# Eight rounds of the last token tile's choice of keys, moved from the value projection into the first half of the attention

## The chip, the cores and the metric

One core of one Trainium2 chip runs the whole program. The metric is device time in microseconds (us). The core's engines run side by side and meet through semaphores: PE (TensorE matmuls), PEld (its weight loads), DVE (VectorE), ACT (ScalarE), POOL (GpSimd) and the DMA queues.

## The reference

Two transformer blocks for 512 tokens of width 1024, in float32: a gated linear attention with a mixture of experts, then an S5 mixer with a dense feed-forward part, then sparse attention with a second one. The change lies in the sparse attention. There, cut to what matters:

```python
score = jnp.einsum('bqhk,bqh->bqk', jax.nn.relu(s_idx), wb)   # 8 index heads
score = jnp.where(causal, score, -jnp.inf)
_, sel = lax.top_k(score, topk)                               # topk = 128
logits = jnp.einsum('bqhd,bqkhd->bhqk', qb, kg).astype(f32) * att_scale
logits = jnp.where(valid, logits, -jnp.inf)
p = jax.nn.softmax(logits, axis=-1).astype(vg.dtype)
return jnp.einsum('bhqk,bqkhd->bqhd', p, vg)                  # 16 heads of 64
```

Each query keeps 128 keys of those at or before it. The 512 queries form four tiles of 128 (t = 0 to 3); tile 0 keeps all its keys, so a choice is made for tiles 1, 2 and 3.

## The kernel before

**The choice.** DVE keeps a score per key in `bias[t]`, 256, 384 or 512 columns wide for t = 1, 2, 3. One round of the choice is MAX8 (L2550: the eight largest of each row) and MATCH_REPLACE (L2551: those eight are marked as taken). Sixteen rounds choose 128 keys; after the sixteenth, L2553 turns marks into a bias of 0 or -1e30. Three tiles make 48 rounds, in the order of tiles. `choose(n)` issues the next n of them at the place where it stands in DVE's program. Nothing but that placement sets their order; DVE works its program off in order, and so do ACT and PE.

**The projections.** A loop over s = 0 to 22. For s up to 20 PE projects one block of index queries, keys or queries, and turns it by the rotary tables (job `rot`, finished by DVE at L2577 and L2580). Steps 21 and 22 are the value projection: each is 96 matmuls of 512 columns, in four halves of 24 (L348, job `dv`). A weight half must be split in two parts before PE uses it: ACT makes the high part (L708), DVE the low part (L716, 128x1024), PE waits for the low part. There are two buffers, used by turns, so ACT may write half g only when PE has begun half g-1, and DVE follows ACT. In steps 21 and 22 DVE goes four times through `weights_low_part` and then `choose`. The two halves that PE starts with in step 21 have been split before; so the first of the four calls splits nothing, and the second splits the third half of the projection.

**The attention.** Each of 64 steps takes one pair (tile, head). Steps 0 to 31 alternate two heads of tile 1 and two of tile 2; the later ones take tiles 0 and 3, the first of tile 3 at step 34. For step s

- PE issues, in this order: the transpose `pt` of pair s-3 (L1370), the product with the values `av` of pair s-4 (L1383), the logits `lg` of pair s (L1392). After the logits of steps 0 to 3 it also issues one filling matmul (L1398) and waits for its end.
- DVE adds the bias to the logits and takes the maximum (L2630, then L2633), in odd steps scales the outputs of pair s-4 (L2600, L2602), and in some steps makes a round of the choice.
- ACT takes the exponential of pair s-1 (L1824), then copies the transpose of pair s-3 out of PSUM (L1834), which `av` of the next step needs.

So the logits of pair s, once DVE has taken their maximum, hold up ACT's exponential, behind that ACT's copy of pair s-2's transpose, and behind that PE's `av` in step s+2. After the attention come the output projection and the second feed-forward part.

Of the kernel before, what the change touches and what calls it, by code (L numbers as in the profile page):

```python
# [140 lines left out]
NR = len(ROPED)  # L141
# [27 lines left out]
NPAIR = len(PAIRS)  # L169
# [223 lines left out]
def block_kernel(nc, io, out, scratch):  # L393

    with ExitStack() as ctx:
# [173 lines left out]
        def free(name):  # L569
            return bank_free[JOBS[name] % 8]  # L570
# [1276 lines left out]
        def _(dve):  # L1847
# [693 lines left out]
            def choose(n):  # L2541

                for _ in range(n):
                    t, at = 1 + chosen[0] // (TOPK // 8), chosen[0] % (TOPK // 8)
                    if t == NTX:
                        return
                    chosen[0] += 1
                    if at == 0:
                        dve.wait_ge(S["b_masked"], t + 1)
                    link(nc.vector.max(m8[:], bias[t]))  # L2550
                    link(nc.vector.match_replace(bias[t], m8[:], bias[t], TAKEN))  # L2551
                    if at == TOPK // 8 - 1:
                        link(nc.vector.tensor_scalar(bias[t], bias[t], TAKEN / 2, MASKED, ALU.is_gt, ALU.mult))  # L2553

            for s in range(NR + 2):
                if s >= NR:
                    for q in range(4):
                        weights_low_part(dve, half_of("dv", s - NR, KT, True) - 2 + q, split_to)
                        choose(4 if s == NR else 3)
                if 1 <= s <= NR and ROPED[s - 1][2] == "tile":  # L2560
                    m = tiles_normed.index(s - 1)
                    dve.wait_ge(S["b_rroot"], norm_index[s - 1] + 1)
                    link(nc.vector.reciprocal(rst[:, m % 2, :], rst[:, m % 2, :]))
                    gain = ROPED[s - 1][3]
                    dve.wait_ge(S["b_raw_ready"], s)
                    nc.vector.scalar_tensor_tensor(out=roped_tile(s - 1), in0=roped_tile(s - 1),
                                                   scalar=1.0 if gain is None else col("qk_gain", gain),
                                                   in1=rst[:, m % 2, :], op0=ALU.mult, op1=ALU.mult) \
                        .then_inc(S["b_normed_q"], 1)
                    dve.wait_ge(S["b_normed_q"], m + 1)  # L2570
                if s < NR:
                    weights_low_part(dve, ahead("dv", ROPED[s][0], ROPED[s][1]), split_to)
                if s >= 2:
                    name = f"rot{s - 2}"
                    ps = result(dve, name)
                    v = roped_tile(s - 2)
                    link(nc.vector.tensor_tensor(rt[:, 0, :], ps[:], cossin[:, 1, :], ALU.mult))  # L2577
                    dve.sem_inc(free(name), 1)
                    dve.wait_ge(S["b_turned_cos"], s - 1)
                    nc.vector.tensor_tensor(v, v, rt[:, 0, :], ALU.add).then_inc(S["b_rotated"], 1)  # L2580
                    dve.wait_ge(S["b_rotated"], s - 1)
                if s == 6:
                    ps = result(dve, "wi")
                    link(nc.vector.tensor_scalar(wi, ps[:, 0:NTX * IH].rearrange("p (t h) -> p t h", h=IH),
                                                 float(IH) ** -0.5, float(HD) ** -0.5, ALU.mult, ALU.mult))
                    dve.sem_inc(free("wi"), 1)
                if s < NR:
                    for t, i in indexed_at(s):
                        index_score(t, i)
                    if s >= INDEX_FIRST + 5:  # L2590
                        choose(4)
# [29 lines left out]
            for s in range(NSTEP):  # L2621
                if s < NPAIR:
                    t, h = PAIRS[s]
                    w = (t + 1) * P
                    b = s % 4
                    name = f"lg{s}"
                    ps = result(dve, name)
                    if s >= 4:
                        dve.wait_ge(bank_done, JB[f"pt{s - 4}"] + 1)
                    link(nc.vector.tensor_tensor_reduce(pp[:, b, 0:w], ps[:, 0:w], bias[t], 1.0, -3.0e38,  # L2630
                                                        ALU.add, ALU.max, mx[:, b:b + 1]))
                    dve.sem_inc(free(name), 1)
                    nc.vector.tensor_scalar(nmx[:, b:b + 1], mx[:, b:b + 1], rsq[:, t, h:h + 1], -1.0, ALU.mult,  # L2633
                                            ALU.mult).then_inc(S["b_logits"], 1)
                if VALUE_LAG <= s < NPAIR + VALUE_LAG and (s - VALUE_LAG) % 2 == 1:
                    outputs_scaled(s - VALUE_LAG)
                if s in TILE_DONE:
                    mixed_low(TILE_DONE[s])
                if s < NPAIR // 2 and s % 4 == 1:
                    choose(1)  # L2640
            assert chosen[0] == (NTX - 1) * (TOPK // 8)
            for j in range(KT):
# [90 lines left out]
```

## Time and profile before

| | |
|---|---|
| runs | 3161.42, 3164.7 and 3247.57 us, median 3164.7 |
| the profiled execution's own time | 3160.65 us |
| its span (first to last instruction) | 3158.8 us, 1.85 us less than its time |
| PE busy | 2900.4 us, 92% of the span |
| DVE busy | 1864.0 us, 59% |
| ACT busy | 1393.9 us, 44% |
| value projection | from 2525.8 to 2579.5 us |
| attention | from 2580.4 to about 2720 us |
| rounds of the choice | from 2513.9 to 2646.3 us |

A timeline row gives start and duration in us, engine, line, operation, output and inputs, the number of instructions, and in brackets how long the engine had sat idle and what ended that. All instants are us from the start of the span.

### The profile page before, as it was taken

To read this page: it belongs to the slowest core of one execution; us is meant where nothing else is said; L and a number is where in the kernel's file an instruction comes from. 1 tells how busy PE (TensorE), PEld (TensorE's weight loads), DVE (VectorE), ACT (ScalarE), POOL (GpSimd) and SP (SyncE) were. 2 spreads that over 40 slices of the span, in tenths; PEclk is the share of its full clock that TensorE was granted. 3 is DMA by queue.
4 is the path that set the end of the run, shared out by engine and by line. 5 is a ranking of instruction groups with operands and counts; after the bars stand their busy time and mean duration, and the time that the engine had idled before them with its cause. 6 is when DMAs were issued, how large, how long until landed. Compare 5 with 4: busy or idle time off the path is not lost.

```text
span 3158.8 us, 35772 instructions
## 1 busy us (share of the span) xinstructions
PE 2900.4 (92%) x12800; PEld 2235.7 (71%) x12800; DVE 1864.0 (59%) x2206; ACT 1393.9 (44%) x1794; POOL 219.7 (7%) x167
## 2 busy tenths in 40 slices
PE   7999999985899999999993678999989999989998
PEld 2548878765677777777772566788867767768887
DVE  3435653564988888888887753333236685343322
ACT  2323233223667777777775323323223435333221
POOL 1100100003930000000001000000001100000000
PEclk9999999996999999999997879999999999999999
DMA  6921722314899989999993802222221110122221
GB/s 236 330 76 60 282 85 94 121 62 161 319 331 352 387 351 387 361 377 369 369 372 108 107 32 75 94 95 106 93 75 67 67 54 1 41 72 101 94 94 67
DMA packets 90801, 546.92 MB, mean 173 GB/s; under 512 B 9232, under 2 KB 18848, under 8 KB 32384
## 3 DMA queue, kind: packets, MB, share of 16 engines
q1 hardware_dynamic: 79584, 485.65, 41.6%
q0 software_dynamic: 10816, 59.58, 5.5%
q8 instruction: 74, 1.21, 0.2%
q14 instruction: 39, 0.32, 0.0%
q10 hardware_dynamic: 288, 0.15, 0.0%
HBM read 516.51 MB, written 41.42 MB: 177 GB/s over the span
## 4 chain that ended last, share of the span: by engine, by line
PE 69%; DVE 17%; issue 6%; DMA 4%; ACT 3%; SPq 1%; POOL 1%; DVEq 0%; ACTq 0%; PEldq 0%; POOLq 0%
PE bank L348 38%; PE bank L286 6%; PE bank L1138 5%; PE bank L1142 4%; PE bank L1141 4%; DVE expert_low L2218 4%; DMA arena<-in_we_stream 2%; ACT expert_high L1587 1%; PE bank L1370 1%; PE bank L1392 1%; PE bank L1383 1%; DMA arena<-in_mod 1%; PE bank L1122 1%; DVE expert_x_low L2303 1%; DVE arena L2320 1%
## 5 line engine op out<-in xcount | busy, mean ns | idle before, releaser
L2218 DVE TENSOR_TENSOR expert_low<-arena,expert_high 128x2048 fp32r<-128x2048 f32 x291 | 684.2, 2382 | 102.7 <-ACT expert_high L1587 85.4
L1587 ACT ACTIVATE expert_high<-arena 128x1024 fp32r<-128x1024 f32 x582 | 597.2, 1057 | 213.4 <-PE bank L1138 117.5
L348 PE MATMUL bank<-high_b,weight_parts 128*128 128x512 f32 x1872 | 592.9, 398 | 29.6 <-DVE low_b L2456 15.9
L716 DVE TENSOR_TENSOR weight_parts<-ring_pages,weight_parts 128x1024 fp32r<-128x1024 f32 x185 | 226.7, 1226 | 557.9 <-ACT weight_parts L708 557.4
L708 ACT ACTIVATE weight_parts<-ring_pages 128x1024 fp32r<-128x1024 f32 x185 | 196.1, 1060 | 591.6 <-PE bank L348 552.4
L348 PEld LDWEIGHTS bank<-high_b,weight_parts 128*128 128x128 f32 x1872 | 352.8, 190 | 121.1 <-issue 36.3
L348 PE MATMUL bank<-low_b,weight_parts 128*128 128x512 f32 x832 | 325.7, 391 | 0.0
L1138 PE MATMUL bank<-expert_high,expert_x_low 128*128 128x512 f32 x768 | 309.5, 403 | 14.1 <-DVE expert_low L2218 10.4
L1141 PE MATMUL bank<-expert_high,expert_x_high 128*128 128x512 f32 x768 | 301.1, 392 | 0.0
L1142 PE MATMUL bank<-expert_low,expert_x_high 128*128 128x512 f32 x768 | 300.6, 391 | 0.0
L348 PE MATMUL bank<-hidden_parts,weight_parts 128*128 128x512 f32 x1056 | 240.0, 389 | 4.3 <-DVE hidden_parts L2502 4.3
L348 PEld LDWEIGHTS bank<-hidden_parts,weight_parts 128*128 128x128 f32 x1056 | 198.0, 188 | 46.3 <-DVE hidden_parts L2502 5.2
L348 PE MATMUL bank<-high_x,parts_a 128*128 128x512 f32 x640 | 202.9, 399 | 9.0 <-DVE parts_a L716 8.6
L1138 PEld LDWEIGHTS bank<-expert_high,expert_x_low 128*128 128x128 f32 x768 | 144.7, 188 | 68.7 <-DVE expert_low L2218 38.2
L348 PEld LDWEIGHTS bank<-low_b,weight_parts 128*128 128x128 f32 x832 | 157.4, 189 | 32.8
L1138 PE MATMUL bank<-expert_high,expert_h_low 128*128 128x512 f32 x384 | 156.2, 407 | 17.5 <-DVE expert_low L2218 15.1
L1142 PEld LDWEIGHTS bank<-expert_low,expert_x_high 128*128 128x128 f32 x768 | 144.9, 189 | 31.8
L1141 PEld LDWEIGHTS bank<-expert_high,expert_x_high 128*128 128x128 f32 x768 | 145.2, 189 | 28.1
L1142 PE MATMUL bank<-expert_low,expert_h_high 128*128 128x512 f32 x384 | 150.3, 391 | 0.0
L1141 PE MATMUL bank<-expert_high,expert_h_high 128*128 128x512 f32 x384 | 149.8, 390 | 0.0
L348 PEld LDWEIGHTS bank<-high_x,parts_a 128*128 128x128 f32 x640 | 122.1, 192 | 35.9 <-issue 9.7
L348 PE MATMUL bank<-high_b,parts_a 128*128 128x512 f32 x320 | 126.7, 396 | 0.0
(464 smaller groups left out, 4033.2 us busy)
## 6 DMA issues: line engine op xcount, KB each, us to landing
arena<-in_we_stream SPq DMA_DIRECT2D x294, 1024.0 KB, 6.5
ring_pages<-in_wb_stream SPq DMA_DIRECT2D x93, 1024.0 KB, 4.8
ring_pages<-in_wa_stream SPq DMA_DIRECT2D x49, 1024.0 KB, 4.9
arena<-in_mod POOLq DMA_DIRECT2D x16, 1024.0 KB
xbuf<-arena POOLq DMA_DIRECT2D x25, 512.0 KB, 15.9
arena<-xbuf SPq DMA_DIRECT2D x17, 512.0 KB, 7.3
ybuf<-arena SPq DMA_DIRECT2D x16, 512.0 KB, 2.6
arena<-kd SPq DMA_DIRECT2D x8, 512.0 KB, 24.1
```

The lines of the kernel that those rows point to most:

```text
L286: ins = pe.matmul(o, lhsT, rhs, start=start, stop=stop)
L348: ins = pe.matmul(o, lhsT, rhs, start=start, stop=stop)
L708: nc.scalar.activation(high, src, ACT.Copy).then_inc(weights_high, 1)
L716: nc.vector.tensor_tensor(low, src, high.bitcast(F32), ALU.subtract).then_inc(weights_split, 1)
L1122: ins = pe.transpose(ps[:, q * P:(q + 1) * P], parts[:, q * P:(q + 1) * P], ident[:])
L1138: ins = pe.matmul(o, low, w_high, start=start, stop=False)
L1141: pe.matmul(o, high, w_high, start=False, stop=False)
L1142: return pe.matmul(o, high, w_low, start=False, stop=stop)
L1370: ins = pe.matmul(ps[:, b * P:(b + 1) * P], pp[:, k % 4, b * P:(b + 1) * P], ident[:], start=True, stop=True)
L1383: ins = pe.matmul(av[:, c:c + HD], pT[:, k % 2, b * P:(b + 1) * P], vt[:, b, h * HD:(h + 1) * HD], start=(b == 0), stop=(b == t))
L1587: nc.scalar.activation(ehigh[c % HIGH_E][:, at], ring_e[c % RING_E][:, at], ACT.Copy) \
L2218: nc.vector.tensor_tensor(elow[c % RING_E][:], ring_e[c % RING_E], ehigh[c % HIGH_E][:].bitcast(F32), ALU.subtract).then_inc(weights_split ...
```

## The change

Two numbers in DVE's program. Before, steps 18, 19 and 20 made 4 rounds each, step 21 four times 4, step 22 four times 3, and the attention one round in steps 1, 5, ..., 29. Now step 21 makes four times 2, and the attention makes a round in every odd step up to 31. In all there are 48 as before.

```diff
@@ -2556,7 +2556,7 @@
                 if s >= NR:
                     for q in range(4):
                         weights_low_part(dve, half_of("dv", s - NR, KT, True) - 2 + q, split_to)
-                        choose(4 if s == NR else 3)
+                        choose(2 if s == NR else 3)
@@ -2636,7 +2636,7 @@
                     outputs_scaled(s - VALUE_LAG)
                 if s in TILE_DONE:
                     mixed_low(TILE_DONE[s])
-                if s < NPAIR // 2 and s % 4 == 1:
+                if s < NPAIR // 2 and s % 2:
                     choose(1)
```

DVE at the start of the value projection, as the first difference between the two programs; L716 here is the low part of the third half (128x256 are rounds of tile 1).

```order
 L2550 MAX m<-arena 128x8
 L2551 MATCH_REPLACE arena<-m,arena 128x256
+L716 TENSOR_TENSOR weight_parts<-ring_pages,weight_parts 128x1024
 L2550 MAX m<-arena 128x8
 L2551 MATCH_REPLACE arena<-m,arena 128x256
```

The third half's low part now stands two rounds of tile 1, and the L2553 that ends them, earlier.

DVE at the end of the value projection, a piece of the difference (128x512 are rounds of tile 3).

```order
-L716 TENSOR_TENSOR weight_parts<-ring_pages,weight_parts 128x1024
-L2550 MAX m<-arena 128x8
-L2551 MATCH_REPLACE arena<-m,arena 128x512
-L2550 MAX m<-arena 128x8
-L2551 MATCH_REPLACE arena<-m,arena 128x512
-L2550 MAX m<-arena 128x8
-L2551 MATCH_REPLACE arena<-m,arena 128x512
 L2577 TENSOR_TENSOR arena<-bank,arena 128x512
 L2580 TENSOR_TENSOR arena<-arena 128x512
```

All eight rounds of tile 3 are gone from here; tile 2's last round now stands ahead of L2577.

DVE in an odd step of the attention that had no round before; the same piece comes again every four steps.

```order
 L2600 RECIPROCAL rsm<-sm 128x2
 L2602 TENSOR_TENSOR arena<-bank,rsm 128x128
+L2550 MAX m<-arena 128x8
+L2551 MATCH_REPLACE arena<-m,arena 128x512
 L2630 ISA arena,mx<-bank,arena 128x256
```

The round stands between the scaling of outputs and the next step's logits.

## Rows read from the trace of the kernel before

**Rows 1.** The page: busy time of PE and the others, share, instructions.
```profile
PE 2900.4 (92%) x12800; PEld 2235.7 (71%) x12800; DVE 1864.0 (59%) x2206; ACT 1393.9 (44%) x1794; POOL 219.7 (7%) x167
```

**Rows 2.** Timeline of PE around the value projection (columns as told above).
```profile
2542.48 0.80 PE L348 MATMUL bank<-weight_parts,low_p 128*128 128x512 f32 x1 [5.24 <-DVE weight_parts L716]
...
2547.62 0.40 PE L348 MATMUL bank<-weight_parts,low_p 128*128 128x512 f32 x1
...
2585.30 1.12 PE L1398 MATMUL bank<-arena,ident 128*128 128x512 f32 x2
2587.94 0.71 PE L1370 MATMUL bank<-ident,arena 128*128 128x128 f32 x4 [1.52 <-ACT arena L1824]
```

**Rows 3.** Timeline of DVE around the value projection.
```profile
2532.99 0.43 DVE L2550 MAX8 m<-arena 128x8 f32<-128x256 f32 x1
...
2541.20 1.23 DVE L716 TENSOR_TENSOR weight_parts<-ring_pages,weight_parts 128x1024 fp32r<-128x1024 f32 x1
...
2579.66 0.70 DVE L2550 MAX8 m<-arena 128x8 f32<-128x512 f32 x1
...
2581.18 0.69 DVE L2550 MAX8 m<-arena 128x8 f32<-128x512 f32 x1
...
2584.21 0.69 DVE L2577 TENSOR_TENSOR arena<-bank,arena 128x512 f32<-128x512 f32 x1
...
2586.36 0.42 DVE L2630 CUSTOM_DVE_ANT_0 arena<-bank,arena 128x256 f32<-128x256 f32 x1
```

**Rows 4.** Timeline of ACT around the value projection.
```profile
2532.06 1.06 ACT L708 ACTIVATE weight_parts<-ring_pages 128x1024 fp32r<-128x1024 f32 x1 [4.34 <-PE bank L348]
2543.38 1.06 ACT L708 ACTIVATE weight_parts<-ring_pages 128x1024 fp32r<-128x1024 f32 x1 [10.25 <-PE bank L348]
```

**Rows 5.** Windows of PE: stretch, length, busy, granted clock, DMA share, GB/s.
```profile
431.50:434.50 3.00, 3.00 (x8) 0.50 0.82 330
```
**Rows 6.** The same view, of the value projection.
```profile
2542.50:2547.00 4.50, 4.50 (x11) 0.50 0.61 233
```

**Rows 7.** Timeline of PE, two other gaps.
```profile
430.43 0.70 PE L348 MATMUL bank<-high_x,parts_a 128*128 128x512 f32 x2 [2.75 <-DVE parts_a L716]
...
434.85 0.63 PE L348 MATMUL bank<-high_x,parts_a 128*128 128x512 f32 x2
```
**Rows 8.** Timeline of PE, a shorter gap.
```profile
2217.24 3.02 PE L348 MATMUL bank<-hidden_parts,weight_parts 128*128 128x512 f32 x12 [2.17 <-DVE hidden_parts L2502]
```

**Rows 9.** Windows of all engines, four steps of the attention: PE, PEld, DVE, ACT, POOL, clock.
```profile
2617.10:2625.25 8.15, 8.15 (x50) 6.02 (x49) 5.03 (x19) 4.27 (x13) 0.00 (x0) 1.00 0.01 2
```

**Rows 10.** Timeline of DVE, steps 15 to 18 of the attention.
```profile
2616.34 0.29 DVE L2602 TENSOR_TENSOR arena<-bank,rsm 128x128 f32<-128x128 f32 x1
2617.15 0.42 DVE L2630 CUSTOM_DVE_ANT_0 arena<-bank,arena 128x256 f32<-128x256 f32 x1 [0.52 <-PE bank L1392]
...
2619.94 0.29 DVE L2602 TENSOR_TENSOR arena<-bank,rsm 128x128 f32<-128x128 f32 x1
2620.38 0.69 DVE L2550 MAX8 m<-arena 128x8 f32<-128x512 f32 x1
...
2621.89 0.56 DVE L2630 CUSTOM_DVE_ANT_0 arena<-bank,arena 128x384 f32<-128x384 f32 x1
```

**Rows 11.** Timeline of ACT, the same steps.
```profile
2618.58 0.47 ACT L1834 ACTIVATE arena<-bank 128x384 f32<-128x384 f32 x1
...
2623.57 0.36 ACT L1834 ACTIVATE arena<-bank 128x256 f32<-128x256 f32 x1
```

**Rows 12.** Timeline of PE, `av` of steps 18, 20 and 32.
```profile
2619.70 0.78 PE L1383 MATMUL bank<-arena 128*128 128x64 f32 x6
...
2623.98 0.66 PE L1383 MATMUL bank<-arena 128*128 128x64 f32 x4
...
2648.89 0.66 PE L1383 MATMUL bank<-arena 128*128 128x64 f32 x4 [0.38 <-ACT arena L1834]
```

**Rows 13.** Timeline of DVE, the end of tile 3's choice.
```profile
2646.34 0.43 DVE L2553 TENSOR_SCALAR arena<-arena 128x512 f32<-128x512 f32 x1
```

## The prediction

> **What bounds the kernel now.** I read the page first: PE is busy for 92% of the span [rows 1], so a change on DVE is worth what it takes from, or adds to, PE's few idle stretches. Then I read the timelines of PE, DVE and ACT from 2500 to 2660 us, where all rounds of the choice lie, and looked for each place where PE's idle time ends with something that DVE did.
>
> There are two near the value projection. PE has worked off two weight halves at 2537.24 (2542.48 less the 5.24 us of idle time in brackets), and waits those 5.24 us for the low part of the third, which DVE starts at 2541.20 and ends at 2542.43 [rows 2, 3]. ACT had made the high part from 2532.06 to 2533.12 [rows 4]: neither the transfer nor ACT is what is late, it is DVE, which from 2532.99 on made eight rounds first. Then PE, at the start of the attention, comes to its first transpose when its last filling matmul ends at 2586.42 and waits 1.52 us for the first exponential, which waits for DVE's first logits at 2586.36 [rows 2, 3]. DVE has no idle time there, it comes straight from tile 3's rounds.
>
> In the attention PE has no idle time: four steps take 8.15 us, PE is busy in all of them and DVE in 5.03 [rows 9]. By its busy share DVE has room for one more round in four steps. What a share does not show is when the round falls. That I read from the starts below.
>
> **Term 1, the stall for the third half.** The low part now stands behind six rounds instead of eight. Six of eight rounds of tile 1 take (2541.20 - 0.33 - 2532.99) x 6/8 = 5.91 us, so it starts at 2538.90, where 0.33 is the last of the eight followed by L2553 (about 0.3 us for 256 columns by the 0.43 of 512 [rows 13]). That is 2.30 us earlier, and PE starts the half at 2540.18. **-2.3 us.** The later halves wait for ACT, which waits for PE: the fourth half's high part began 0.90 us after PE began the third [rows 2, 4], took 1.06, and DVE's low part takes 1.23: some 3.3 us with the hand-overs, where a half of 24 matmuls takes PE 24 x 0.227 = 5.4. With two or three rounds (2.5 to 3.8 us) between the low parts, DVE is in time for every one of them, so the gain is kept to the end of the projection. DVE will have idle time in the first half of it, which costs nothing.
>
> **Term 2, the clock behind that stall.** In the gap the granted clock falls to 0.50, its lower level of 1.2 GHz [rows 6], and PE needs 5.14 us for the 12 matmuls from 2542.48 to 2547.62 [rows 2]; at the upper level they take 12 x 0.227 = 2.72 (0.227 from three in 0.68 us). So 2.4 us are lost. The new gap is 2540.18 - 2537.24 = 2.94 us. The nearest rows are a gap of 2.75 us, after which the clock was at 0.50 too, and twelve matmuls took 4.42 us, from 430.43 to 434.85, 1.7 more than at the upper level [rows 5, 7]; and a gap of 2.17 us, after which 12 matmuls took 3.02 including the last one's tail, at the upper level throughout [rows 8]. 2.94 is nearer to 2.75 and beyond it, so I take 1.7 lost instead of 2.4: **-0.7 us.** The ends are 0 lost (-2.4) and 3.4 lost, twice as long at the low level (+1.0).
>
> The Trainium skill ("TensorE: Matmul & The Clock Gate", section "Why this matters for your kernels") advises short idle gaps between bursts of matmuls, so that the clock is not taken back, and by its advice the shortened gap would just pass. By that rule the clock term would be the end of -2.4, not -0.7. The row of the 2.75 us gap speaks against it, that of 2.17 us for it.
>
> **Term 3, the first exponential.** Without tile 3's eight rounds (1.52 us each, from 2579.66 to 2581.18 [rows 3]) DVE would be at its first logits 12.2 us sooner; but L2577 ahead of them waits for PE's last rotation, which comes 3.0 us sooner by terms 1 and 2. From there DVE has L2577, L2580, a reciprocal, 2586.36 - 2584.21 = 2.15 us in all, and starts the logits at about 2580.5, 5.9 us before its former time. Exponential and hand-overs take 2587.94 - 2586.36 = 1.58 us, so PE could have it at 2582.1, and comes to it at 2586.42 - 3.0 = 2583.4. The wait goes: **-1.5 us.** Here PE would be 4.5 us ahead of before.
>
> **Term 4, the eight rounds in the attention.** Steps 1, 5, ... have had theirs; new are steps 3, 7, ..., 31. Look at step 15. DVE scales outputs at 2616.34 and is free for a round 0.44 us later (2619.94 to 2620.38 in the step that has one); the round holds it for 1.51 (2620.38 to 2621.89) [rows 10]. The next logits, ready at 2617.15, then start at 2616.34 + 0.44 + 1.51 = 2618.29: 1.14 us late. ACT's exponential waits for them, and behind it in ACT's order its copy, which before ended at 2618.58 + 0.47 = 2619.05, ends at 2620.19 [rows 11]. PE's `av` of step 18 began at 2619.70 [rows 12] and needs that copy; with a hand-over of 0.06 it begins at 2620.25. PE is late by **0.55 us**. That this coupling is real can be seen twice before the change: the round of step 17 makes the copy end at 2623.93 and `av` begin at 2623.98; and where L2553 follows the last round (0.46 us more), PE stands idle 0.38 us at 2648.89 [rows 11 to 13].
>
> The lag does not pile up on DVE (it stays ahead of PE over four steps), but each such round sets PE back anew. Steps 7, 11, 15, 19, 23 and 27: 6 x 0.55 = 3.3 us. Step 3 has a filling matmul behind it and no outputs to scale, which covers its round: 0. Step 31 has the last round and L2553: its next logits are late by 1.14 + 0.46 and, since tile 0's logits are ready some 0.2 to 0.3 us sooner, 1.9 in all; less the slack of 0.59 (2619.70 - 2619.05 - 0.06) that is 1.3, while the stall at 2648.89, with L2553 gone from step 29, goes (0.38 and a little over 0.1 of late start): +0.8. Together **+4.1 us**. The ends: 0, if ACT's copy had more room than the rows show; and 8 x 1.51 = 12.1, if nothing at all were covered. I take 4.1, since it comes from the starts themselves.
>
> **The sum.** -2.3 - 0.7 - 1.5 + 4.1 = -0.4 us, on the profiled execution's own 3160.65: 3160.2. Its time lies 0.8 us under the lowest and 4.05 us under the median of the runs shown. From the lowest run, 3161.4, it is 3161.0. I take 3161.0 as the time to be measured. A measurement of this kernel can tell 2%, 63 us, from no change; no case below comes near it.
>
> **The rivals.**
>
> *The clock stays up* (as with the 2.17 us gap [rows 8]). -2.3 - 2.4 - 1.5 + 4.1 = -2.1: 3159.3. For it, that the gap shrinks by almost half; against it, the 2.75 us gap.
>
> *The rounds hide in the attention.* DVE is idle for 3.1 of 8.15 us [rows 9], and 1.51 fits in. If ACT's copy did not wait behind the exponential, the sum would be -4.5: 3156.9. Against it, the two places of rows 12 where PE already follows a late copy.
>
> *Slower: DVE's round sits whole in PE's path.* In the steps with a new round, DVE is 1.14 us late for the logits; if PE's transposes or the release of PSUM banks also waited for it, each of eight rounds would cost up to its whole 1.51 us: +12.1 - 4.5 = +7.6, 3169. It decides from the point where DVE's late logits are still late four steps on, that is if the four steps of DVE, 5.03 + 1.51 = 6.5 us of work and its hand-overs, took over 8.7. In between, at a cost of 1.14 for each of seven, +3.5: 3165.
>
> *The change does not do what it says:* the third half waits for something else, say the ring page or PE's own buffer. Then terms 1 and 2 are nothing, term 3 stays, and the sum is +2.6: 3164. Against it, ACT's high part done at 2533.12, nine microseconds early [rows 4].
>
> **How the numbers follow.** Forecast 0.55, clock up 0.15, rounds hidden 0.1, rounds wholly in the path 0.12 (most of it the milder price), no gain at the half 0.03; 0.05 for what I have not seen. The range reaches from the hidden rounds' 3156.9, a little lower for the spread between runs, to the milder slower case with 2 us of that spread: 3156.5 to 3167. It leaves out the 3169 case and most of what is unseen. Faster or slower by over 2% would need 63 us, for which no case has a mechanism: 0.01 and 0.02, the rest within.
>
> **What the profile of the changed kernel would show.** PE's gap in front of the third half about 2.9 us, still ended by L716 (term 1); granted clock 0.50 after it for a stretch shorter than before, or not at all (term 2). No idle time ahead of the first L1370 (term 3), and the last filling matmul some 3 us earlier. In the attention, idle time of PE of 0.5 to 0.65 us ahead of L1383, ended by ACT L1834, six times, 8.7 us (8.15 + 0.55) apart, and one of about 1.3 near step 34 (term 4); PE's lead over before shrinks from 4.5 us at step 9 to almost nothing at step 34, and stays so to the end. I am wrong if the lead at step 34 is over 2 us, or if PE's lag in four steps is over 1 us.

## The result, and the profile after

No difference of 2% from the kernel before can be told, and the time is not the one that was forecast. The ratio to the kernel before is 1.0076, with a 95% interval of 1.0051 to 1.0100. The median of 20 executions is 3197.3 us, outside the forecast range of 3156.5 to 3167.

This ratio can't be understood alone: the comparison leaves out executions more than 1.5% above the fastest of their kernel, and so leaves out those of before near 3247 us (12 of 20) but keeps those of the changed kernel near 3200 us (13 of 20). All executions taken together show this:

| | to 3180 us | 3180 to 3230 | over 3230 | mean of all |
|---|---|---|---|---|
| before, 20 beside the changed kernel | 8, median 3165.3 | 0 | 12, 3238 to 3257 | 3214.3 |
| changed, 20 | 7, median 3167.3 | 13, 3192 to 3207 | 0 | 3188.2 |
| before, all 167 of this study | 103, median 3164.3 | 2 | 62 | 3195.5 |

Each kernel, then, has two kinds of execution. The profile tells what the second kind is in the changed kernel. The page of the changed kernel, busy times and the granted clock in 40 slices, is of an execution of 3193.91 us:

```profile
span 3192.1 us, 35771 instructions
PE 2939.2 (92%) x12800; PEld 2262.0 (71%) x12800; DVE 1864.8 (58%) x2206; ACT 1395.3 (44%) x1794; POOL 219.5 (7%) x167
PEclk9999999996999999999998699999999996899999
```

PE is busy 39 us longer than in [rows 1], with as many instructions, and DVE for 0.8. PE's timeline shows the three places that the prediction spoke of: the third half, the first transpose, and `av` of steps 10, 14 and 34 (bracket: idle time and what ended it).

```profile
2539.27 0.50 PE L348 MATMUL bank<-weight_parts,low_p 128*128 128x512 f32 x1 [2.95 <-DVE weight_parts L716]
...
2543.70 0.39 PE L348 MATMUL bank<-weight_parts,low_p 128*128 128x512 f32 x1
...
2582.69 0.68 PE L1370 MATMUL bank<-ident,arena 128*128 128x128 f32 x4 [0.30 <-ACT arena L1824]
...
2586.57 0.70 PE L1392 MATMUL bank<-arena 64*128 64x256 f32 x2
...
2598.54 0.88 PE L1383 MATMUL bank<-arena 128*128 128x64 f32 x6 [0.38 <-ACT arena L1834]
...
2607.34 0.88 PE L1383 MATMUL bank<-arena 128*128 128x64 f32 x6 [0.57 <-ACT arena L1834]
...
2647.50 0.48 PE L1392 MATMUL bank<-arena 64*128 64x128 f32 x2
...
2651.74 1.05 PE L1383 MATMUL bank<-arena 128*128 128x64 f32 x6 [1.14 <-ACT arena L1834]
...
2676.02 1.95 PE L1370 MATMUL bank<-ident,arena 128*128 128x128 f32 x8
```

Against the kernel before this trace starts the stall 0.91 us sooner (2542.48 - 5.24 against 2539.27 - 2.95, the last digit rounded), for reasons that lie ahead of the change. With that taken off, PE is 2.3 us ahead at the third half, and 5.40 - 0.91 = 4.5 us ahead at the logits of step 4 (2591.97 before, 2586.57 now), as forecast. At `av` of step 34 (2652.34 before, 2651.74 now) the lead has been used up and 0.3 us more. From there to the end of the program the changed kernel loses 33.9 us, and all of it before the output projection, whose first matmuls start 33.3 us later (first line before, second now) behind the same wait of 1.89 us:

```profile
2726.11 0.74 PE L348 MATMUL bank<-high_b,weight_parts 128*128 128x512 f32 x2 [1.89 <-DVE low_p L2616]
```
```profile
2759.40 0.74 PE L348 MATMUL bank<-high_b,weight_parts 128*128 128x512 f32 x2 [1.89 <-DVE low_p L2616]
```

No new wait does it. Windows of the changed kernel, the first three of PE alone (length, busy, granted clock, DMA share, GB/s): behind the stall for the third half, in the first half of the attention, and behind `av` of step 34. The last two, of all engines in the second half of the attention, give PE, PEld, DVE, ACT, POOL and then the clock:

```profile
2540.20:2543.00 2.80, 2.80 (x8) 0.50 0.97 328
...
2600.00:2640.00 40.00, 37.54 (x221) 1.00 0.01 1
2654.00:2664.00 10.00, 9.34 (x31) 0.50 0.01 2
```
```profile
2680.00:2700.00 20.00, 20.00 (x70) 15.39 (x70) 5.08 (x25) 6.92 (x21) 0.00 (x0) 0.50 0.01 1
2700.00:2720.00 20.00, 20.00 (x66) 14.87 (x66) 5.07 (x24) 5.99 (x18) 0.00 (x0) 0.50 0.00 1
```

and of the kernel before (all engines):

```profile
2680.00:2700.00 20.00, 19.67 (x114) 14.29 (x112) 9.05 (x42) 11.08 (x33) 0.00 (x0) 1.00 0.01 1
```

The clock was granted at 0.50, the level of 1.2 GHz, right behind the gap of 1.14 us, came back for some steps, and fell again, to the end of the attention, at the transposes of 2676.02 us: eight matmuls that start there take 1.95 us, those at 2666.74 took 1.16. At 0.50 PE works off 70 matmuls in 20 us instead of 114. In the trace of the kernel before the clock stays at 1.00 through the attention.

### The profile page after: what moved, and what is told of

It reads as the page before. It is cut to its first block, busy times and chain, and to the rows that moved or that the text cites. A ratio compares the mean times of both kernels' runs of the same rounds, so it can differ in the third digit from the quotient of the medians.

```text
span 3192.1 us, 35771 instructions
## 1 busy us (share of the span) xinstructions
PE 2939.2 (92%) x12800; PEld 2262.0 (71%) x12800; DVE 1864.8 (58%) x2206; ACT 1395.3 (44%) x1794; POOL 219.5 (7%) x167
## 4 chain that ended last, share of the span: by engine, by line
PE 70%; DVE 16%; issue 6%; ACT 3%; DMA 3%; SPq 1%; POOL 0%; DVEq 0%; ACTq 0%; PEldq 0%; POOLq 0%
PE bank L348 40%; PE bank L286 6%; PE bank L1138 4%; DVE expert_low L2218 4%; PE bank L1142 4%; PE bank L1141 4%; DMA arena<-in_we_stream 2%; PE bank L1392 2%; ACT expert_high L1587 1%; PE bank L1370 1%; PE bank L1383 1%; PE bank L1122 1%; DVE expert_x_low L2303 1%; DVE arena L2320 1%; PE bank L1194 1%
## 5 line engine op out<-in xcount | busy, mean ns | idle before, releaser
L716 DVE TENSOR_TENSOR weight_parts<-ring_pages,weight_parts 128x1024 fp32r<-128x1024 f32 x185 | 226.7, 1226 | 561.3 <-ACT weight_parts L708 560.9
```

The source lines that it names most:

```text
L716: nc.vector.tensor_tensor(low, src, high.bitcast(F32), ALU.subtract).then_inc(weights_split, 1)
```

## The experiments

Seventeen kernels ran, most of them 12 times, one (evenf2, again as evenf2b) twice 12 times. What is counted is the number of executions over 3180 us and over 3230 us; one over 3180 us is said to have fallen. In the traces kept, those from 3180 to 3230 us had a low clock in the second half of the attention, and the one over 3230 us, of proj, in the whole of it. No trace of the kernel before near 3247 us was kept; its executions there, beside the experiments, have a mean clock over the span of 0.924 to 0.932, like proj's 0.929; those to 3180 us have 0.954 to 0.962. "Even rounds" is the version with `s % 2 == 0` for `s % 2` in the attention.

The expectations name their theories by letters. G: idle gaps of PE bring the clock down. A: the sparse steps, with tile 0's small matmuls, do it by themselves. P: it hangs on where in time these steps lie. M: it falls without regard to gaps. R: a round costs the same wherever it stands.

| kernel | runs | to 3180 (median) | 3180 to 3230 | over 3230 |
|---|---|---|---|---|
| before | 167 | 103 (3164.3) | 2 | 62 |
| changed | 20 | 7 (3167.3) | 13 | 0 |
| proj: term 1 alone | 12 | 9 (3165.9) | 0 | 3 |
| att: terms 3 and 4 | 12 | 7 (3166.4) | 5 | 0 |
| bfill: before + 1 filling matmul | 12 | 12 (3165.4) | 0 | 0 |
| bfill64: the same, other data | 12 | 11 (3163.6) | 1 | 0 |
| no31: last round in the projection | 12 | 8 (3163.6) | 4 | 0 |
| afterf2: changed + 2 filling | 12 | 7 (3170.2) | 5 | 0 |
| afteralt: changed, other order | 11 | 11 (3171.4) | 0 | 0 |
| less, lessf1: eight rounds left out | 6 and 6 | 0 | 12 | 0 |
| even rounds | 12 | 4 (3158.1) | 8 | 0 |
| evenf1, +1 filling | 12 | 8 (3159.5) | 4 | 0 |
| evenf2 and evenf2b, +2 filling | 24 | 22 (3163.7) | 2 | 0 |
| evenf3, +3 filling | 12 | 7 (3164.5) | 5 | 0 |
| even35, filling at step 35 | 12 | 7 (3161.9) | 5 | 0 |
| evenfill4, at 35, 41, 47, 53 | 12 | 5 (3161.8) | 7 | 0 |
| evenswap | 7 | 2 (3173.3) | 5 | 0 |
| evenalt: other order | 12 | 10 (3164.0) | 2 | 0 |

(One more execution of proj took 5877 us; it is unlike all others and not counted. The bound of 3180 us is a reading aid, and shorter falls lie under it: evenswap's execution of 3178.7 us had a low clock for 51 us, evenf2b's of 3174.7 us for about 30.)

The rows come from several chips, and on these the kernel before, run beside each row, was not alike: 15 of 30 over 3230 us beside proj, even, no31 and less; 10 of 30 beside bfill, evenswap, even35 and evenfill4; 9 of 30 beside evenf1, evenf2, lessf1 and att; 10 of 29 beside bfill64, afterf2 and evenf3; 6 of 28 beside evenalt, afteralt and evenf2b. A difference between rows of different groups may in part be one of chips.

**The first transpose and the executions near 3247 us.**

proj, term 1 without the rest:

```diff
-                        choose(4 if s == NR else 3)
+                        choose((2, 6, 4, 4)[q] if s == NR else 3)
```

> Term 1 alone, with all rounds in the projection that were there before: step 21 makes 2, 6, 4, 4 rounds instead of 4, 4, 4, 4, the attention is as before. The third half comes 2.3 us sooner, the fourth at its former time, so PE reaches the attention about 1.5 us sooner, but DVE its first logits at the former time, 2586.4. Expected: the gap of 1.5 us ahead of the first L1370 grows to about 3 us and the time stays at 3160.6, 0 us from before, where the clock stays up. Theory G: with a gap of 3 us at the beginning of the attention the clock falls there in at least as many executions as before, and such an execution loses most of the attention's 130 us at half clock: some 80 us, 3240. Rival M: no more and no fewer such executions than before.

Ratio 1.0003 (0.9992 to 1.0014). The third half came in time (gap 2.94 us), but two later gaps of 1.32 and 1.10 us took its place, both ended by L716, so PE came to the first transpose no sooner, with a gap of 1.51 us and not the 3 of the forecast. Term 1 alone is worth nothing. 3 of 12 were over 3230 us, where theory G had at least the share of the kernel before (15 of 30). Its profile, of an execution of 3250.9 us span, is the one in which the clock fell at the beginning. PE's timeline there, and the windows (all engines) of the stretch behind it:

```profile
2594.98 1.11 PE L1370 MATMUL bank<-ident,arena 128*128 128x128 f32 x4 [1.51 <-ACT arena L1824]
```
```profile
2596.00:2650.00 54.00, 53.70 (x170) 38.39 (x170) 17.57 (x67) 16.95 (x45) 0.00 (x0) 0.50 0.00 1
2650.00:2720.00 70.00, 70.00 (x230) 51.26 (x229) 22.87 (x87) 21.22 (x56) 0.00 (x0) 0.50 0.00 1
```

Four transposes that took 0.71 us in [rows 2] take 1.11: the clock is down right behind the gap, and stays at 0.50 for the whole attention, although PE is busy nearly all of the time.

bfill puts work into that gap:

```diff
     if _s < FILLED:
         JOBS_B += [f"fill{_s}"]
+    if _s == 2:
+        JOBS_B += ["fill2b"]
...
+                if s == 2:
+                    ps = opened("fill2b")
+                    pe.matmul(ps[:], ident[:], vt[:, 0, 0:512], start=True, stop=True).then_inc(bank_done, 1)
+                    pe.wait_ge(bank_done, JB["fill2b"] + 1)
+                    pe.sem_inc(free("fill2b"), 1)
```

> The kernel before with one filling matmul more, after the one of step 2, where PE waited 1.52 us for the first exponential: PE has 1.4 us of work in place of the wait, so the path does not change. Theory G (a gap of 1.5 us at the beginning of the attention brings the clock down for the whole of it): no execution near 3247 us is left of those that before had in half its cases (27 of 50); the best ones stay at 3160 to 3166 us. Where the clock then falls in the second half instead, an execution takes about 3195 us, as the changed kernel's do. Rival M (no tie to the gap): executions near 3247 us as often as with the kernel before.

Ratio 1.0013 (1.0004 to 1.0023); but 0 of 12 over 3180 us, with 12 of 30 of the kernel before on the same chip. PE's timeline (two filling matmuls in a row, then the transpose) and its windows:

```profile
2594.50 1.13 PE L1400 MATMUL bank<-arena,ident 128*128 128x512 f32 x2
2595.77 1.10 PE L1405 MATMUL bank<-arena,ident 128*128 128x512 f32 x2
2597.17 0.68 PE L1372 MATMUL bank<-ident,arena 128*128 128x128 f32 x4 [0.30 <-ACT arena L1831]
```
```profile
2596.00:2650.00 54.00, 53.40 (x307) 1.00 0.01 1
...
2669.20:2672.40 3.20, 3.17 (x15) 0.51 0.00 0
2673.00:2730.00 57.00, 56.23 (x339) 1.00 0.00 1
```

307 matmuls in 54 us where proj had 170. Behind the gap of step 36 the clock fell here too, but came back after some 3 us. In all, no kernel whose gap ahead of the first transpose was 0.9 us or less had an execution over 3230 us (0 of 206); those with 1.5 us had 65 of 179. It does not take a filling matmul: att and the changed kernel close the gap without one more (0 of 32). That much is shown: the gap of term 3 is what costs 80 us, in about a third of the executions, and closing it is worth far more than its 1.5.

**Where the rounds stand.**

att, the changed attention with the old third half:

```diff
-                        choose(2 if s == NR else 3)
+                        choose(4 if s == NR else 1)
```

> The attention of the changed kernel alone: sixteen rounds in its odd steps, but the eight are taken out of step 22 (four times 1 instead of 3), and step 21 keeps four times 4. The third half is as late as before (gap of 5.24 us), the first exponential is in time. By the terms: -1.5 (term 3) + 4.1 (term 4) = +2.6 us, 3163.3 us at a clock of 1.00, six gaps of 0.57 us and one of 1.14. No execution near 3247 us, since the gap of 1.52 us ahead of the first transpose is gone. How many fall in the second half tells whether it hangs on the inside of the attention (then as with the changed kernel, 13 of 20, theory G) or on its place (theory P: another share, as the attention begins 2.9 us later than in the changed kernel).

No execution over 3230 us, the best at 3162.0 and the median of seven at 3166.4, 0.7 above the 3165.7 of the kernel before on that chip, where 2.6 were forecast; in the second half the clock fell in 5 of 12. PE's waits from 2575 to 2660 us (total, times, longest):

```profile
PE bank L1383 <- ACT arena L1834: 4.6, 7, 1.1
```

The same line, with the same numbers, stands in the changed kernel's waits: term 4's seven gaps, without term 1. In this trace, of 3168.9 us, the clock stayed at 1.00 behind the gap of 1.14 us, behind which it fell in the changed kernel's.

even, the sixteen rounds moved by one step:

```diff
-                if s < NPAIR // 2 and s % 2:
+                if s < NPAIR // 2 and s % 2 == 0:
```

> The sixteen rounds of the attention in its even steps (0, 2, ..., 30) instead of the odd ones; the projection as in the changed kernel. Theory G (the gaps): PE's 0.57 us gaps come from rounds that stand in front of the logits of steps 8, 12, ...; in an even step there is no scaling of outputs ahead of the round, so the logits of the next step are late by 0.3 us at most and ACT's copy is in time. Expected: gaps ahead of L1383 gone but for one of about 0.6 us at step 33, PE 4.7 us ahead of before at step 34, and, since no gap of 1.1 us is left in the attention, a granted clock of 1.00 through it: 3156 us. Rival R (term 4 is too small because rounds cost DVE time wherever they stand): same gaps, 3161 us. Rival M (the clock falls in the attention without regard to gaps): gaps gone, but many executions near 3190 us or more as before.

The gaps went, as expected. PE's waits there:

```profile
PE bank L1392 <- DVEq L759: 1.1, 1, 1.1
PE bank L1383 <- ACT arena L1834: 0.8, 2, 0.5
```

The four executions to 3180 us have a median of 3158.1 against 3164.1 of before's: 6.0 us less, where 4.7 were worked out. In the trace PE needs 63.97 us from the first transpose to `av` of step 34 (2582.94 to 2646.91), before 64.40 (2587.94 to 2652.34). So the rounds cost PE nothing in an even step: rival R is out. But the clock fell all the same, in 8 of 12, as M had it and against G (one gap of 1.11 us was left, at step 36, which the kernel before has too). In its profile PE stands idle nowhere for over 0.35 us between 2653.36 and the fall:

```profile
2665.69 0.48 PE L1392 MATMUL bank<-arena 64*128 64x128 f32 x2
2666.10 1.96 PE L1370 MATMUL bank<-ident,arena 128*128 128x128 f32 x8
```

These are the same transposes, of step 43, as at 2676.02 us in the changed kernel: tile 3's, behind four pairs of tile 0.

no31 takes away the gap in step 34:

```diff
-                        choose(2 if s == NR else 3)
+                        choose(2 if s == NR else 4 if q == 3 else 3)
...
-                if s < NPAIR // 2 and s % 2:
+                if s < NPAIR // 2 - 1 and s % 2:
```

> The changed kernel with the round of step 31, the last of all, made at the end of step 22 instead. Theory G: the 1.14 us gap ahead of L1383 in step 34 goes, replaced by nothing; the six gaps of 0.57 us stay. PE 1.4 to 1.5 us further ahead at step 34: 3159 us at a clock of 1.00. If the 1.14 us gap is what brings the clock down at 2652 us, no execution falls there any more and none lies near 3200 us. Rival M: executions near 3200 us stay as frequent as with the changed kernel (13 of 20), falling elsewhere.

The gap went, and one of 0.90 us ahead of the first transpose, not forecast, came, as DVE reached the attention 1.5 us later. 4 of 12 fell, against 13 of 20: fewer, yet the gap in step 34 is not the only cause (with so few executions the two shares are not far enough apart to be sure of more).

less leaves out the eight added rounds (tile 3 keeps 64 keys, L2553 follows its eighth round):

```diff
-                if s < NPAIR // 2 and s % 2:
+                if s < NPAIR // 2 and s % 4 == 1:
```

> The changed kernel without its eight additional rounds in the attention (rounds in steps 1, 5, ..., 29 only). It leaves out the last eight rounds of tile 3's choice, so that tile keeps only 64 keys; L2553 is still done. This is terms 1 to 3 alone. Theory G: 3160.65 - 4.5 = 3156 us, PE 4.4 us ahead of before at step 34, only gaps of 0.1 and one of 0.4 us in the attention, and a clock of 1.00 throughout. If it falls in the attention nonetheless, gaps are not what brings it down (rival M), and times near 3190 to 3240 appear.

6 of 6 fell, 3189 to 3202 us, though no gap of the added rounds was left. The forecast failed, and with it theory G as an account of the added gaps: whether these have a part in the 13 of 20 is not shown. Its windows of PE:

```profile
2590.00:2650.00 60.00, 59.14 (x350) 1.00 0.00 1
2661.00:2700.00 39.00, 39.00 (x132) 0.50 0.00 1
```

**Gap, sparse steps, place or data.**

evenswap, outputs scaled ahead of the logits:

```diff
             for s in range(NSTEP):
+                if VALUE_LAG <= s < NPAIR + VALUE_LAG and (s - VALUE_LAG) % 2 == 1:
+                    outputs_scaled(s - VALUE_LAG)
                 if s < NPAIR:
...
-                if VALUE_LAG <= s < NPAIR + VALUE_LAG and (s - VALUE_LAG) % 2 == 1:
-                    outputs_scaled(s - VALUE_LAG)
```

> Rounds in the even steps, and DVE scales the outputs of pair s-4 ahead of the logits of step s instead of behind them. In step 35 this frees the PSUM bank that the logits of step 36 wait for, so the gap of 1.11 us there (ended by DVE's release of a bank) should go or fall under 0.4 us, and the gap of 0.53 us in step 33 with it. At a clock of 1.00: 1 to 1.5 us less than the even rounds alone (best 3157.4), 3156. If the 1.11 us gap is what brings the clock down in the second half (theory G), the executions between 3184 and 3206 us (8 of 12 with the even rounds) become few; if low activity of the steps of tile 0 does it by itself (rival A), they stay about 2 in 3.

A miss. DVE now waited in odd steps for `av` of the same step before it could take the logits; with that, gaps of 0.60 and 0.95 us ahead of `av` came back, and behind the one of 0.95 the clock fell already in the first half:

```profile
2619.89 0.66 PE L1383 MATMUL bank<-arena 128*128 128x64 f32 x4 [0.95 <-ACT arena L1834]
...
2621.11 1.56 PE L1370 MATMUL bank<-ident,arena 128*128 128x128 f32 x6
```

even35 and evenfill4 put filling matmuls into the second half:

```diff
-    if _s < FILLED:
+    if _s < FILLED or _s == 35:
...
-                if s < FILLED:
+                if s < FILLED or s == 35:
```

(evenfill4: `in (35, 41, 47, 53)`.)

> Rounds in the even steps and one filling matmul after the logits of step 35, which takes PE 1.4 us where it waited 1.11 us: +0.3 us at a clock of 1.00, so the best executions at 3158. Theory G for the second half: executions over 3184 us become few, as PE is busy in the gap. Rival A: the clock still falls at the transposes of step 43, as it did in the profile of the even rounds (at 2666.1 us, no gap over 0.25 us in the 10 us ahead of it), and 2 of 3 executions stay between 3184 and 3206 us.

> Rounds in the even steps and a filling matmul after the logits of steps 35, 41, 47 and 53, so that each stretch of tile 0's small matmuls has 1.1 us of dense work: 4 x 1.4 us less the waits that they replace (1.1 and some 0.2 each), about +4 us at a clock of 1.00: 3161. Rival A (low activity of these steps brings the clock down): here the executions over 3184 us go or become few, and the median over all executions is near 3162. If they stay, neither the gap nor the sparse steps explain the fall.

5 and 7 of 12 fell, where the even rounds had 8. Filling the 1.11 us gap does not keep the clock, nor does dense work of 1.1 us between the sparse stretches. A window of even35 has PE recorded as busy without a break, at the low clock:

```profile
2666.00:2735.00 69.00, 69.00 (x216) 0.50 0.00 1
```

evenf1, evenf2, evenf3 and evenf2b move the attention later by one, two or three filling matmuls of 1.42 us after step 2 (names `fill2b`, `fill2c`, `fill2d` in the form of bfill's edit, on the even rounds):

> Rounds in the even steps and one filling matmul more after step 2, where PE waits for nothing any more: the whole attention from step 3 on comes 1.42 us later than with the even rounds, its inside is the same. Theory P (position): whether the clock falls in the second half depends on where in time its sparse steps lie, which is nearly the same in every execution; the change moved them 4.2 us forward, onto a bad place, and 1.4 us back brings them to where the kernel before with one more filling matmul had them (0 of 12 executions over 3173 us). Expected: 3157.5 + 1.4 = 3159 us for the best and nearly all executions under 3172 us, against 4 of 12 without the filling matmul. Theory G or A (gaps or sparse steps by themselves): 8 of 12 between 3184 and 3206 us as before, since no gap in the attention has changed.

> The same with two more filling matmuls: attention 2.84 us later than with the even rounds. At a clock of 1.00 3160.3 us. Theory P gives another share of executions over 3184 us than either 0 or 1 more (which, it does not say, as no kernel so far had this place); theories G and A give the same share as for the even rounds, 2 in 3.

> The even rounds with three more filling matmuls: 4.26 us later, so that the attention begins where it began in the kernel before, which fell in its second half in 2 of 43 of the executions that had not fallen at the first transpose. At a clock of 1.00: 3157.5 + 4.3 = 3162 us. Theory P: few or none over 3184 us. If the number of filling matmuls mattered through their work and not through the shift, also none; if neither, 2 in 3.

> The even rounds with two more filling matmuls once more. If the 0 of 12 over 3184 us is the kernel's own: again 0 or 1 of 12, median 3162 us. If it was chance out of a share like the 5 or 8 of 12 of its neighbours with three or none: 3 or more of 12.

With 0, 1, 2, 2 again and 3 of them 8, 4, 0, 2 and 5 of 12 fell. The inside of the attention, from the first transpose to `av` of step 34, is the same to 0.03 us. None against two (8 of 12 against 2 of 24) is far from chance, if the difference of the chips is left aside. So what lies ahead of the attention seems to matter; but that it is the place in time is not shown. Theory P forecast nearly none with one and with three, and 4 and 5 fell; evenf2b's 2 lie between its two forecasts; and its own trace has the clock low from 2690 to 2720 us. The instants speak against P too: the two traces of the same kernel, evenf2 and evenf2b, begin the third half at 2534.00 and 2538.17 us, and bfill and bfill64, alike up to there, at 2551.66 and 2543.45. The executions lie further apart than the shifts of 1.42 us, so a place counted from the start of the program cannot decide it. The filling matmuls are also more dense work, a rival that no run separates.

afterf2, the changed kernel with two:

> The changed kernel, rounds in its odd steps, with two more filling matmuls after step 2: the attention with all its gaps (six of 0.57 us, one of 1.14) comes 2.84 us later. At a clock of 1.00: 3160.2 + 2.8 = 3163 us. Theory P (place): far fewer than 13 of 20 over 3184 us, near the 0 of 12 of the even rounds with two. Theory G (gaps inside): as many as with the changed kernel, about 8 of 12.

5 of 12, against 2 of 24 with the gaps gone and 13 of 20 without the filling matmuls. The numbers are too small to say which of the two counts, or both.

lessf1 and bfill64. lessf1 is less with bfill's edit. bfill64 is bfill with

```diff
-                    link(nc.vector.match_replace(bias[t], m8[:], bias[t], TAKEN))
+                    link(nc.vector.match_replace(bias[t], m8[:], bias[t], TAKEN if t < 3 or at < 8 else -1.0e38))
```

> The changed kernel without its eight additional rounds in the attention (tile 3 keeps only 64 keys), and one filling matmul more after step 2. Without the filling matmul 6 of 6 executions lay between 3189 and 3202 us. Its attention is step for step that of the kernel before with one more filling matmul, only 2.8 us sooner in the program. Theory P: with the 1.42 us shift most executions come to 3158 to 3165 us. Theory G or A: 6 of 6 over 3184 us again.

> The kernel before with one more filling matmul, every instruction the same and at the same place, but the last eight rounds of tile 3 mark their keys with a value that does not count as taken: tile 3 keeps 64 keys instead of 128, so that more of its softmax weights are zero. Nothing but data differs. If data plays no part in the clock, executions lie at 3160 to 3173 us (0 of 12 over 3173 without this edit). If the sparser data makes the clock fall or stay down in tile 3's steps, most lie between 3187 and 3203 us, and the two kernels with rounds left out (6 of 6 there) are explained by their data and say nothing on gaps or place.

lessf1 fell 6 of 6, against theory P; bfill64 1 of 12. So the data, half of tile 3's keys, is not what made less and lessf1 fall. Up to `av` of step 34 the attentions of lessf1 and bfill64 differ by one wait of PE of 0.19 us, at 2633.64 us; what else differs lies ahead of the attention. In both the clock dips at step 36's gap for some 3 us and comes back; in lessf1 it falls again 10 us after that dip began (granted 1.00 from 2665 to 2671 us, 0.50 behind it). Why the one does and the other doesn't stays open.

evenalt and afteralt spread the small steps out:

```diff
-for _order in ((1, 2) * (AH // 2), (0, 3, 0) * (AH // 4) + (3,) * (AH // 4)):
+for _order in ((1, 2) * (AH // 2), (0, 3) * (AH // 2)):
```

> Rounds in the even steps, and the second half of the attention takes two heads of tile 0 and two of tile 3 by turns all the way, instead of four of tile 0 after two of tile 3 and eight pairs of heads of tile 3 at the end. Same work. Theory A (a stretch of four small pairs in a row brings the clock down): no execution over 3184 us, best ones 3156 to 3162 us. If the stretch is not what does it: about 8 of 12 over 3184 us as with the even rounds.

> The changed kernel with the same order of the second half. At a clock of 1.00 the gap of 1.14 us in step 34 stays, so 3160 to 3168 us. Theory A: few over 3184 us instead of 13 of 20. If the gaps that the rounds make (0.57 us six times, 1.14 us in step 34) are enough by themselves: about 8 of 12 over 3184 us.

2 of 23 over 3180 us, where the same kernels in the old order had 21 of 32. Neither forecast was met to the letter: evenalt has the 2 (3189.2 and 3195.7 us) where none was expected, and 7 of afteralt's 11 lie above its 3160 to 3168 us, up to 3178.7. In afteralt's profile the clock still fell behind the 1.14 us gap, and came back, but for one more dip of about 3 us at step 36. Its windows:

```profile
2659.00:2665.00 6.00, 6.00 (x21) 0.50 0.02 4
2673.00:2730.00 57.00, 55.50 (x326) 1.00 0.00 1
```

That fits a reading in which the gaps bring the clock down and the stretches of tile 0's small matmuls keep it down or let it fall again. For the falls of the second half it is the only forecast whose share held for both kernels. It is not shown beyond that: on the same chip evenf2b, in the old order, fell in 2 of 12 as well, the kernel before was over 3230 us least often there, and neither kernel ran in the old order without filling matmuls on that chip.

**A version better than both.** By the mean over all executions: bfill 3165.7 us (before in the same comparison 3192.5), evenf2 and evenf2b 3167.5 together (3189.4 and 3182.8), evenalt 3168.3 (3182.8), changed 3188.2 (3214.3). Among executions to 3180 us the even rounds are the fastest, with a median of 3158.1. None differs from before by 2%. The gain of all of them is that the executions near 3247 us don't occur; evenf2 and the spread order had, besides, few near 3195.

## Why the prediction was wrong

**Term 1, the stall: right.** Forecast -2.3; the gap is 2.95 us instead of 5.24.

**Term 2, the clock behind it: right in this trace, in part by luck.** The low level was there from 2540.2 to 2543.0 us; the first 12 matmuls of the third half take 4.43 us, from 2539.27 to 2543.70, against 2.72 at the upper level: 1.7 us lost, as I took. The rule of the Trainium skill ("TensorE: Matmul & The Clock Gate", section "Why this matters for your kernels"), by which the shortened gap would have kept the clock, did not hold here: behind the gap of 2.95 us the clock fell, as it did behind those of 1.51 and 1.14 us in the attention. How long the low level lasts differs from trace to trace, so the agreement is in part luck: of the 16 traces with a gap of 2.93 to 2.95 us there, 11 have the low level until some 3.5 us behind the start of the third half, 4 until some 5.6 (evenf2, evenf2b, evenalt, afterf2), and evenswap not at all.

**Term 3, the first exponential: the mechanism right, its worth wrong.** The 1.52 us wait is down to the 0.30 of the filling matmul's hand-over. I priced the wait at its own length. With bfill it is seen to be worth some 80 us in the 62 of 167 executions of the kernel before that lie over 3230 us.

**Term 4, the rounds: right, a little small.** From the logits of step 4 to `av` of step 34 before took 60.4 us, now 65.2: +4.8, where I had 4.1. The six rounds whose price I had at 0.55 us cost 0.66 in the mean: the gaps are 0.38, 0.57, 0.57, 0.74, 0.57 and 0.57 us, some 8.8 us apart, and to each comes a slower start of the matmuls behind it. The step 31 case (1.3 forecast) shows 1.14 idle, in the sum with step 34's start +0.85 where I had +0.8. DVE's and ACT's starts are those worked out: in the changed trace the round stands at 2603.87, the next logits 1.52 us later at 2605.39, ACT's copy at 2606.82, PE at 2607.34:

```profile
2603.87 0.69 DVE L2550 MAX8 m<-arena 128x8 f32<-128x512 f32 x1
2605.39 0.43 DVE L2630 CUSTOM_DVE_ANT_0 arena<-bank,arena 128x256 f32<-128x256 f32 x1
2606.82 0.47 ACT L1834 ACTIVATE arena<-bank 128x384 f32<-128x384 f32 x1
```

So the lead is 4.5 us at step 4 and nothing at step 34, which the last part of the prediction had asked for. Had the clock stayed up, the sum would be -2.3 - 0.7 - 1.5 + 4.8 = +0.3 us; the two kernels' executions at the high clock are 1.9 us apart in the median (3167.3 and 3165.3), within their own spread of 5 to 8.

**What failed is the step from the sum to the time.** The sum was put on the profiled execution and the lowest run, both of the kind with the attention at a clock of 1.00, and the 3247.57 of the three runs shown got no place in it, while 12 of the 20 executions beside the changed kernel (62 of all 167) are of that kind, with the attention at 1.2 GHz. In the prediction the clock was a term at the third half only; for the gaps that term 4 opens (seven, the last of 1.14 us) and the one that term 3 closes I wrote lengths and no clock. Rows 9 had the clock at 1.00 and I carried that over to a kernel with other gaps. That clock term inside the attention was put at nothing without a reason; in the changed kernel's trace it measures 33.9 us, between `av` of step 34 and the output projection. No rival had the clock falling inside the attention, so the range could not hold 3197. Why the changed kernel falls in its second half in 13 of 20 executions, where the kernel before did in 2 of the 105 that were under 3230 us, stays open: less fell in 6 of 6 without the added rounds and their gaps.

**The rivals.** The clock did not stay up behind the third half in the changed kernel's trace; the rounds did not hide; they did not sit whole in PE's path; the third half did wait for DVE's L716. The slower time came by a way that none of them named.

## What to carry to other kernels

Where TensorE works off many small matmuls, price a gap by what the clock does behind it, not by its length: 1.5 us cost 80 here in about a third of the executions, and a filling matmul in the gap, free by the path, took that away. Filling the later gap of 1.11 us did not help, so try it and count. Read the times of all runs before the profile, and if they fall into groups, find the granted clock of each group before adding up terms. And when moving work on a helper engine, place it by the starts of the chain, not by busy share: the same sixteen rounds make PE 4.8 us later at step 34 when they stand behind the odd steps' outputs, and no later in the even steps.

## What the runs showed of the hardware

- The granted clock fell to 0.50 behind PE's gap of 2.93 to 2.95 us ahead of the third half in 15 of the 16 traces that have it, and stayed at 1.00 in evenswap. Behind gaps in the attention it did so in some traces and not in others: with 1.51 us (proj) but not with 1.52 (before), with 1.14 us (changed) but not in att; once with 0.95 us (evenswap). Behind gaps of 1.32 and 1.10 us between the dense matmuls of the value projection (proj) it stayed at 1.00.
- In the attention it stayed there with PE recorded busy without a break: 69.00 of 69.00 us in even35, 70.00 of 70.00 in proj. In bfill, bfill64 and evenf2 it came back there after some 3 us. In the dense matmuls of the third half it came back within 5.7 us of their start. The busy share of the records does not tell which of the two will happen.
- It fell with no gap over 0.35 us in the 12 us ahead of it (even, 2666.10 us), behind four pairs of tile 0.
- Open: why less and lessf1 fell in 12 of 12 and bfill and bfill64, with nearly the same attention, in 1 of 24; why there were fewer falls with two filling matmuls ahead than with three; and how much of either is the chip's.
